# Second joint of a two-block kernel: the new x's sum of squares taken from three sums beside the down projection

## What is computed

```python
# end of the first block
h = rmsnorm(x, g_ffn_pre[l]) * (1.0 + scale_f) + shift_f
f = (jax.nn.silu(h @ w_gate[l]) * (h @ w_up[l])) @ w_down[l]
x = x + gate_f * rmsnorm(f, g_ffn_post[l])
# start of the second block
h = h + hybrid_mixer(rmsnorm_2(h, norm_mix_w[i]), w_in[i], ...)
# rmsnorm and rmsnorm_2
y = xf * lax.rsqrt(jnp.mean(xf * xf, axis=-1, keepdims=True) + EPS)
```

## Time and profile before

| what | value |
|---|---|
| median of three runs | 1722.43 us |
| the profiled execution's own time | 1722.28 us |
| its span, first to last instruction | 1720.5 us |
| mean granted TensorE clock | 0.994 |
| TensorE busy | 1694.8 us, 99% of the span |
| VectorE, ScalarE, GpSimd busy | 751.5, 712.6, 785.7 us |

### The profile page before, as it was taken

How to read it: one execution, slowest core, us unless ns; L and a number is a source line. 1 busy time by engine, 2 the same in 40 slices (tenths; PEclk the granted TensorE clock), 3 DMA queues, 4 the chain that set the end, 5 groups by cost and what they waited for, 6 DMA issues and landing times.

```text
span 1720.5 us, 22097 instructions
## 1 busy us (share of the span) xinstructions
PE 1694.8 (99%) x8054; PEld 1375.9 (80%) x8054; DVE 751.5 (44%) x1146; ACT 712.6 (41%) x963; POOL 785.7 (46%) x612
## 2 busy tenths in 40 slices
PE   6999999999999999999999999999999999999998
PEld 4777798888888888888888888887888788888887
DVE  6777744111110036567778778666114222222002
ACT  4565455222233345334434636445223444433232
POOL 3324244444446663544443344345444444444663
PEclk8999999999999999999999999999999999999999
DMA  7655322222213323422323232223233222222332
GB/s 256 218 185 176 118 84 77 98 98 89 97 59 101 94 76 135 137 98 86 112 97 98 100 108 99 95 79 98 98 120 113 92 91 90 92 98 72 93 92 74
DMA packets 55300, 184.61 MB, mean 107 GB/s; under 512 B 5920, under 2 KB 8224, under 8 KB 54720
## 3 DMA queue, kind: packets, MB, share of 16 engines
q1 hardware_dynamic: 55232, 183.67, 31.9%
HBM read 179.39 MB, written 4.26 MB: 107 GB/s over the span
## 4 chain that ended last, share of the span: by engine, by line
PE 93%; DVE 4%; ACT 2%; issue 1%; DMA 0%; SPq 0%; DVEq 0%; ACTq 0%
PE PR L558 26%; PE PR L557 26%; PE PR L561 26%; PE AX L1041 1%; PE PR L572 1%; PE PR L573 1%; PE PR L571 1%; DVE macc L1716 1%; PE AX L791 1%; PE AX L1045 1%; PE AX L594 1%; PE AX L765 1%; PE AX L775 1%; PE AX L602 1%; PE AX L1030 1%
## 5 line engine op out<-in xcount | busy, mean ns | idle before, releaser
L497 POOL TENSOR_TENSOR wlo<-raw,whi 128x512 fp32r<-128x512 f32 (+1 forms) x600 | 779.5, 1323 | 883.5 <-ACT whi L1169 883.5
L1169 ACT ACTIVATE whi<-raw 128x1024 fp32r<-128x1024 f32 x288 | 301.7, 1051 | 136.9 <-PE PR L561 132.4
L557 PE MATMUL PR<-h3h,whi 128*128 128x512 f32 x608 | 245.7, 404 | 0.0
L558 PE MATMUL PR<-h3l,whi 128*128 128x512 f32 x608 | 240.6, 396 | 0.0
L561 PE MATMUL PR<-h3h,wlo 128*128 128x512 f32 x608 | 154.2, 396 | 0.0
L557 PE MATMUL PR<-h4h,whi 128*128 128x512 f32 x351 | 139.5, 397 | 0.0
L558 PE MATMUL PR<-h4l,whi 128*128 128x512 f32 x351 | 138.8, 396 | 0.0
L561 PEld LDWEIGHTS PR<-h3h,wlo 128*128 128x128 f32 x608 | 114.4, 188 | 27.5
L558 PEld LDWEIGHTS PR<-h3l,whi 128*128 128x128 f32 x608 | 114.6, 189 | 26.3 <-issue 1.0
L557 PEld LDWEIGHTS PR<-h3h,whi 128*128 128x128 f32 x608 | 114.4, 188 | 26.5 <-issue 1.2
L557 PE MATMUL PR<-h2h,whi 128*128 128x512 f32 x320 | 126.9, 397 | 0.1
(11 more groups left out here) (368 smaller groups left out, 2986.6 us busy)
## 6 DMA issues: line engine op xcount, KB each, us to landing
raw<-w SPq DMA_DIRECT2D x224, 512.0 KB, 3.5
cond<-wcond SPq DMA_DIRECT2D x48, 512.0 KB, 4.9
raw<-w SPq DMA_DIRECT2D x32, 384.0 KB, 3.1
raw<-w SPq DMA_DIRECT2D x32, 320.0 KB, 2.8
abc_a<-acum_rows SPq DMA_DIRECT2D x8, 512.0 KB, 3.9
abc_b<-acum_rows SPq DMA_DIRECT2D x8, 512.0 KB, 4.3
x<-xin SPq DMA_DIRECT2D x2, 1024.0 KB, 7.9
x_keep<-x SPq DMA_DIRECT2D x1, 2048.0 KB, 7.3
```

The lines of the kernel that those rows point to most:

```text
L497: ins = pool.tensor_tensor(wlo[:, j, a:a + n], raw[:, j, a:a + n], whi[:, j, a:a + n], ALU.subtract)
L557: pe.matmul(bank, whi[:, j, w], oh[:, k0 + k, :], start=first and i == 0, stop=False)
L558: pe.matmul(bank, whi[:, j, w], ol[:, k0 + k, :], start=False, stop=False)
L1169: act.activation(whi[:, j, :], raw[:, j, :], ACT.Copy).then_inc(hi_ready, 1)
```

## The change

For halves 2 and 3 the sum of squares of x' = x + r g y is put together from three sums: that of x x, that of x g y, and that of g y g y, as (gsq r + 2 cross) r + xx, and cut off at 0 from below.

- The sum of x x is taken from PSUM bank AX 3, where the first joint left it for the same x.
- The other two are gathered beside the down projection. For each finished piece ScalarE writes (g y) squared into `sqx`, and VectorE writes x g y into another part of `sqx` and adds both into `abc_a` (here `cross_sum` and `gsq_sum`). These are three more VectorE instructions and one more ScalarE instruction for each of the nine pieces. The loops over pieces are written out.
- TensorE sums them over partitions in `gate_sum`: for half 2 in the last tile's second half, for half 3 before k = 5 of `first_units`, where `mix_sum(3)` now stands as well. `x_sum(2)` and `x_sum(3)` are gone, and ScalarE's sixteen squares of the new x with them.
- VectorE puts the sum together in five instructions (`whole`), each waiting for the one before, and ScalarE makes the scale from it (`whole_rms`). r now lies in SBUF (`rr`), before it lay in PSUM.
- VectorE no longer adds all eight steps and then makes h. `half_both` goes tile by tile: step, h of the tile before, addition, low part. Piece 8 and `whole(3)` stand within the first half's loop.
- ScalarE's program has `whole_rms(2)` between `hi` of units 100 and 101, and one h tile between `hi` of 101 and 102.
- In `first_units` the second half takes unit 103 into the k loop, so that four units are released together at its end.

The core of the diff:

```diff
         def step_half(q, k):
 
-            bank = PR[:, 3, :] if q == JOINTS - 1 else AX[:, 1, :]
-            return bank[:, HALF[k % 2]]
+            return AX[:, 1, HALF[k % 2]] if q < 2 else AX[:, 3, HALF[0]]
+
+        cross_sum, gsq_sum = abc_a[:, 0, :], abc_a[:, 1, :]
+
+        def gsq(n, c):
+
+            return sqx[:, 2 * (n % 2):2 * (n % 2) + 2, :].rearrange("p a b -> p (a b)")[:, 0:c.stop - c.start]
+
+        def cross(c):
+
+            return sqx[:, 4:6, :].rearrange("p a b -> p (a b)")[:, 0:c.stop - c.start]
+
+        def whole_sum(q):
+
+            return sqx[:, 4 + q, :]
+
+        def gate_sums(q):
+
+            bank = AX[:, 1, :] if q == 2 else PR[:, 3, :]
+            return bank[:, HALF[0]], bank[:, HALF[1]]
...
+            def gate_sum(q, n):
+
+                c, (at_cross, at_gsq) = HALF[q % 2], gate_sums(q)
+                pe.wait_ge(cross_acc, n + 1)
+                pe.matmul(at_cross, con_("ones"), cross_sum[:, c], start=True, stop=True)
+                pe.wait_ge(gsq_acc, n + 2)
+                pe.matmul(at_gsq, con_("ones"), gsq_sum[:, c], start=True, stop=True).then_inc(three_done, 1)
...
@@ -931,13 +959,13 @@
                     for k in range(nk):
                         if e == 1 and j == 0 and k == 4:
                             mix_sum(2, V_DN1 + N_DN - 1)
-                        mm = strip(j, fh1, fl1, k0, k, PR[:, 1 + e, :], c, j == 0 and k == 0, j == 3 and k == nk - 1)
+                        if e == 1 and j == 1 and k == 2:
+                            gate_sum(2, N_DN - 1)
+                        mm = strip(j, fh1, fl1, k0, k, PR[:, 1 + 2 * e, :], c, j == 0 and k == 0, j == 3 and k == nk - 1)
                     if e == 1:
                         mm.then_inc(unit_used, 1)
                 if e == 0:
                     mm.then_inc(half_done, 1)
-            x_sum(2)
-            mix_sum(3, V_DN1 + N_DN)
...
+                    own = range(4 if e == 1 else 3)
                     for k in range(KT):
+                        if e == 0 and k == 5:
+                            mix_sum(3, V_DN1 + N_DN)
+                            gate_sum(3, N_DN)
                         pe.wait_ge(hh_ready, KT + KT * (2 + e) + k + 1)
                         pe.matmul(AX[:, 1, c], wdt2[:, 64 * k:64 * k + P], h3h[:, k, c], start=k == 0, stop=False)
-                        for j in range(3):
+                        for j in own:
                             if e == 0 and k == 0:
                                 pe.wait_ge(lo_ready, U_SC + j + 1)
                             with_high(j, h3h, k, c)
@@ -966,16 +998,15 @@
                         mm = pe.matmul(AX[:, 1, c], wdt2[:, 64 * k:64 * k + P], h3l[:, k, c], start=False, stop=k == KT - 1)
                         if e == 1 and k == KT - 1:
                             mm.then_inc(dt_done, 1)
-                        for j in range(3):
+                        for j in own:
                             mm = with_low(j, h3l, k, c)
                             if e == 1 and k == KT - 1:
                                 mm.then_inc(unit_used, 1)
                     if e == 0:
-                        x_sum(3)
                         pe.wait_ge(lo_ready, U_SC + 4)
-                    for k in range(KT):
-                        mm = strip(3, h3h, h3l, 0, k, PR[:, 3, :], c, k == 0, k == KT - 1)
-                mm.then_inc(unit_used, 1)
+                        pe.wait_ge(u_ready, 2)
+                        for k in range(KT):
+                            strip(3, h3h, h3l, 0, k, PR[:, 3, :], c, k == 0, k == KT - 1)
...
+            def gate_rms(q):
+
+                c, n = HALF[q % 2], 2 * q + 2
+                act.wait_ge(ss_ready, q + 1)
+                act.activation(AX[:, 0, c], AX[:, 0, c], ACT.Ln, bias=vec_("eps", 0), scale=1.0 / D).then_inc(ln_ready, 1)
+                act.wait_ge(ln_ready, n)
+                act.activation(rr[:, c], AX[:, 0, c], ACT.Exp, scale=-0.5).then_inc(r_ready, 1)
+
+            def whole_rms(q):
+
+                n = 2 * q + 3
+                act.wait_ge(u_ready, q - 1)
+                act.activation(r_half(q), whole_sum(q), ACT.Ln, bias=vec_("eps", 0), scale=1.0 / D).then_inc(ln_ready, 1)
+                act.wait_ge(ln_ready, n)
+                act.activation(r_half(q), r_half(q), ACT.Exp, scale=-0.5).then_inc(r_ready, 1)
...
+            act.wait_ge(mod_ready, 7)
+
             def down_piece(n):
                 m, c = PIECES_DN[n]
                 act.wait_ge(*((half_done, 5) if n == KT - 1 else (unit_used, U_DN1 + 4 * m + 4)))
-                keep(n % 2, V_DN1 + n - 1, PR[:, (0, 1, 2)[n - 6], :], mix2[:, m, :], c)
-
-            with act.Fori(0, KT // 2 - 1) as i:
-                for b in range(2):
-                    for j in range(4):
-                        hi(i, 8, U_DN1 + 4 * b + j + LEAD)
-                    act.wait_ge(unit_used, 8 * i + (U_DN1 + 4 * b + 4))
-                    keep(b, 2 * i + (V_DN1 + b - 1), PR[:, b, :], tile(mix2, 2 * i + b), slice(0, T))
+                keep(n % 2, V_DN1 + n - 1, PR[:, m % 2 if n < 7 else (1, 3)[n - 7], :], mix2[:, m, :], c)
+                act.wait_ge(mix_ready, R0 + N_OUT + n + 1)
+                act.wait_ge(gsq_acc, n + 1)
+                act.activation(gsq(n, c), mix2[:, m, c], ACT.Square, scale=gffn[:, m:m + 1]).then_inc(gsq_ready, 1)
+
+            for n in range(6):
+                for j in range(4):
+                    hi(0, 4, U_DN1 + 4 * n + j + LEAD)
+                down_piece(n)
             for j in range(4):
                 hi(0, 4, U_DN1 + 24 + j + LEAD)
             down_piece(6)
             hi(0, 4, U_DN1 + 28 + LEAD)
             down_piece(7)
-            mix_rms(2)
+            gate_rms(2)
             hi(0, 4, U_SC)
-            x_squares(2, (0, 1))
+            whole_rms(2)
             hi(0, 4, U_SC + 1)
-            x_squares(2, (2, 3, 4))
+            split_half(2, h3h, (0,))
             hi(0, 4, U_SC + 2)
-            x_squares(2, (5, 6, 7))
+            split_half(2, h3h, (1,))
             down_piece(8)
-            x_rms(2)
-            split_half(2, h3h, (0, 1))
-            mix_rms(3)
-            split_half(2, h3h, (2,))
+            split_half(2, h3h, (2, 3))
             hi(0, 4, U_SC + 3)
-            split_half(2, h3h, range(3, KT))
-            x_squares(3, range(KT))
-            x_rms(3)
+            split_half(2, h3h, (4, 5))
+            gate_rms(3)
+            split_half(2, h3h, (6,))
+            whole_rms(3)
+            split_half(2, h3h, (7,))
             split_half(3, h3h, range(KT))
...
 
             def down_piece(n):
+
+                m, c = PIECES_DN[n]
                 add_piece(PIECES_DN, n, N_OUT, V_DN1)
+                dve.wait_ge(mix_ready, R0 + N_OUT + n + 1)
+                dve.wait_ge(cross_acc, n + 1)
+                dve.scalar_tensor_tensor(cross(c), mix2[:, m, c], gffn[:, m:m + 1], x[:, m, c], ALU.mult,
+                                         ALU.mult).then_inc(cross_ready, 1)
+                dve.wait_ge(cross_ready, n + 1)
+                dve.tensor_tensor(cross_sum[:, c], cross_sum[:, c], cross(c), ALU.add).then_inc(cross_acc, 1)
+                dve.wait_ge(gsq_ready, n + 1)
+                dve.wait_ge(gsq_acc, n + 2)
+                dve.tensor_tensor(gsq_sum[:, c], gsq_sum[:, c], gsq(n, c), ALU.add).then_inc(gsq_acc, 1)
+
+            def whole(q):
+
+                c, u, (at_cross, at_gsq), at = HALF[q % 2], whole_sum(q), gate_sums(q), 4 * (q - 2)
+                dve.wait_ge(r_ready, 2 * q + 2)
+                dve.wait_ge(three_done, q - 1)
+                dve.tensor_tensor(u, at_gsq, rr[:, c], ALU.mult).then_inc(u_step, 1)
+                dve.wait_ge(u_step, at + 1)
+                dve.scalar_tensor_tensor(u, at_cross, 2.0, u, ALU.mult, ALU.add).then_inc(u_step, 1)
+                dve.wait_ge(u_step, at + 2)
+                dve.tensor_tensor(u, u, rr[:, c], ALU.mult).then_inc(u_step, 1)
+                dve.wait_ge(u_step, at + 3)
+                dve.tensor_tensor(u, u, AX[:, 3, c], ALU.add).then_inc(u_step, 1)
+                dve.wait_ge(u_step, at + 4)
+                dve.tensor_scalar(u, u, 0.0, None, ALU.max).then_inc(u_ready, 1)
+
+            def half_both(q, beside=lambda k: None):
+
+                c = HALF[q % 2]
+
+                def step(k):
+                    if k >= 1:
+                        dve.wait_ge(res_ready, KT * q + k)
+                    dve.scalar_tensor_tensor(step_half(q, k), mix2[:, k, c], gffn[:, k:k + 1], rr[:, c], ALU.mult,
+                                             ALU.mult).then_inc(upd_ready, 1)
+
+                def residual(k):
+                    dve.wait_ge(upd_ready, KT * q + k + 1)
+                    dve.tensor_tensor(x[:, k, c], x[:, k, c], step_half(q, k), ALU.add).then_inc(res_ready, 1)
+
+                def full(k):
+                    dve.wait_ge(*(h_low(q, k - RING) if k >= RING else h_low(q - 1, k + RING)))
+                    dve.wait_ge(res_ready, KT * q + k + 1)
```

(41 more changed lines are left out.)

## The result

The changed kernel takes 1726.48 us (median of 15 runs, 1724.78 to 1729.37), the kernel before, run beside it, 1722.34 (15 runs, 1720.65 to 1724.32). The ratio is 1.0024, with a 95% interval from 1.0018 to 1.0031: slower by 4.1 us, of which the interval leaves 3.1 to 5.3. The forecast was 1726.0.

What follows compares the result with a forecast made beforehand. TensorE, busy 99% of the span, was taken as the bound. Unit 104 2.5 us later plus 1.1 for the clock gave 1722.28 + 3.6 = 1725.9 profiled, 1726.0 as median; range 1722.7 to 1728.9.

Steps and rivals of the forecast that it cites:

- Passes: On TensorE, 32 records of sums drop out and 8 are added, 5.2 us less to do.
- Down projection: Added VectorE and ScalarE instructions per piece are hidden behind TensorE's passes; `gate_sum(2)` starts at 626.6 and nothing waits.
- Weights: At the start of half 2, low parts of unit 102 come late; TensorE stands still until 638.9 instead of 637.19.
- VectorE in half 2: VectorE needs 1.44 us a tile plus 0.6 for contention, TensorE 1.3; TensorE goes on at 649.9 after low part 6.
- I take 0.3: Extra us for a VectorE step with two SBUF inputs beside GpSimd in half 2, bounded by 0 and 0.5.
- The end: At the end of `first_units`, TensorE pauses 1.9 us before unit 104, waiting for its high part.
- The clock: TensorE's clock falls to half around the pause at half 2's start, some 6.8 us in all, costing 1.1 us.
- x_keep: Starts near 662 instead of 649.6; unit 105's weights behind it land at 672, hidden with 3 us to spare.
- The sum: Unit 104 starts 2.5 us later, plus 1.1 for the clock: 3.6 us later in all.
- Light: Rival: in half 2 contention costs 0 to 0.15 and the clock holds, +0.7 to +1.6 us; chance 0.33.
- faster: Rival: VectorE keeps up with TensorE in half 2 and weights come in time, -4.2 us; chance 0.04.
- Heavy: Rival: contended instructions cost 0.5, GpSimd 0.2; VectorE ends half 2 two us later, +4.9 or +6.5; chance 0.18.

Runs made afterwards that it cites:

- products in pauses: Changed kernel plus 33 unused products of the dt weights in TensorE's three pauses at the start of half 2: 1726.70 us.
- old order: Changed kernel, but VectorE does all eight steps and additions of a half first, then multiplies and low parts: 1739.81 us, one run.
- unit 103 behind: Changed kernel with unit 103's products of the second half behind the k loop again, as in the kernel before: 1724.43 us.
- no low parts: GpSimd makes low parts of only 64 of 1024 weight columns for units 100 to 103: changed kernel 1721.67 us, kernel before 1722.11 us.
- all cures: Changed kernel with weights' high parts early, unit 103's strips behind the k loop, r in PSUM, steps 0 and 1, piece 8 and half 3's sums reordered: 1723.80 us.

## Why the prediction was right, point by point

Times count from `mix_sum(2)`; for the prediction that is 624.76.

- **Passes**: 24 records fewer, as said. **Down projection**: `gate_sum(2)` 1.84 us behind `mix_sum(2)`, forecast 1.84. Nothing waited there.
- **Weights**: high parts of 101 and 102 at 5.9 and 8.2, forecast 6.5 and 8.2; TensorE released at 13.4, forecast 14.1. The times are near, but the waits did not set the end: the chain passes them by on VectorE, and no run shows a price for them.
- **VectorE in half 2**: the mechanism was right, its size was off. The step that failed is "I take 0.3" for a contended instruction: it is 0.37 to 0.55, 0.47 in the mean (5.2 us over 11). The upper bound of 0.5 held for most. "Its contended price is nowhere in the trace" was too much said: the row at 633.66 above had the 0.47, for an addition instead of a step, and the low part's 0.34 was the poorer guide. Behind h tile 0, which was there 0.1 early, tiles 0 to 3 took 8.7 us (8.2 forecast: eight contended instructions at 0.3, where six were, at 0.47), piece 8 took 3.0 (2.4), and the low part of tile 6 released TensorE at 26.0 instead of 25.1.
- **The end**: the pause is 1.86 us, 1.9 forecast, released by ScalarE.
- **The clock**: it fell as forecast, for 6.9 us, and not in the last pause, though in two of the other kernels with that pause it did, behind unit 104 (products in pauses, old order). Its price of 1.1 us was wrong for this execution, where it was 0: what I let "vanish in the waits for VectorE" was only 0.6, and it was all of it. In the execution with unit 103 behind it was 1.36. So the price depends on when the clock falls, which the prediction's one number did not allow for.
- **x_keep** stayed hidden: from unit 104 to 700 us TensorE waited for nothing more.
- **The sum**: +3.6 forecast, 3.59 measured. That is two errors that cancel, 1.1 too much for the clock and 0.9 too little for VectorE, with 0.2 on the way to unit 104; so close an agreement is luck. Light is out by the contended price, faster by VectorE's time for a tile, 1.45 us even without GpSimd (no low parts, 633.30 to 634.75). Heavy, with 0.5 and VectorE hiding the clock, described this execution better than the forecast did, but put VectorE two us later where it was 0.9. Its +4.9 is excluded by the measure, not by the device times, whose interval goes to 5.3.

By the rule of the Trainium skill (page "SBUF — State Buffer", section "Who interferes with whom") the prediction estimated the mean wait at half a GpSimd pass, 0.36. The runs show 0.47. A possible reason is that the two engines do not meet at random moments: VectorE's next such instruction is ready again when GpSimd's next pass, queued without a gap, has just begun. That reading is argued from the durations and was not tested by itself.

## What to carry to other kernels

Saving passes of the busiest engine pays only where its feeders keep up: the same three sums win 2.6 us in the half where VectorE has time and lose in the half where GpSimd works beside it. Before an operand is moved from PSUM to SBUF, count the VectorE instructions that then read two SBUF tensors while GpSimd is at work: they took twice their time here, and one more Exp that kept a copy in PSUM undid it. And price a pause or a fall of the clock only after asking which engine is last there: 6.9 us at half clock, about 4 of them work of TensorE, cost nothing where VectorE was last, and 3.3 us of TensorE's work at half clock cost 1.5 us where TensorE was.

## What was not expected of the hardware

- The low parts (L2123 in the changed kernel, two SBUF inputs) fell from a median of 0.78 us to 0.52 in the kernel with all cures, though GpSimd worked beside them and their own operands had not changed. What an instruction loses to GpSimd seems to depend on how its neighbours have set the two engines against each other; several other instructions had moved in that kernel too, so the reason stays open.
- When the clock falls, relative to the program, differs between executions: 10.2 us behind `mix_sum(2)` in the changed kernel, some 13.5 in the one with unit 103 behind, though both run the same instructions up to there. A single profile can so hide or show over 1 us (there 1.36), so a difference of that size between two profiles has to be checked against the medians, and the windows of both read for the clock, behind the measured stretch as well.
- The same instructions up to `mix_sum(2)` reached it between 623.65 and 626.44 us. Differences of this size are to be read inside the joint, not from the span.
